# A two-block network on one core: the S5 recurrence over 64 chunks of 8 steps, its matrices formed in the first feed-forward block

## The reference

```
lam_bar = exp(lam * dt);  b_bar = (lam_bar - 1) / lam * B
hs[t] = lam_bar * hs[t-1] + b_bar @ u[t]        # complex, per group
y[t]  = real(C @ hs[t]) + d * u[t]
g = gelu(y);  val, gate = split(g @ w_glu + b_glu);  out = val * sigmoid(gate)
```

## Time and profile before

| | |
|---|---|
| Time, median of 3 runs | 3404.18 us (3403.97 to 3410.24) |
| The profiled execution | 3402.89 us, its span 3401.1 us |
| PE busy | 3106.1 us, 91% of the span |
| DVE, ACT, POOL busy | 1746.6, 1050.0, 1472.9 us |
| Moved by DMA | 280.1 MB, mean 82 GB/s |

### The profile page before, as it was taken

How to read it: one execution, slowest core, us unless ns; L and a number is a source line. 1 busy time by engine, 2 the same in 40 slices (tenths; PEclk the granted TensorE clock), 3 DMA queues, 4 the chain that set the end, 5 groups by cost and what they waited for, 6 DMA issues and landing times. The chain is left out here.

```text
span 3401.1 us, 42283 instructions
## 1 busy us (share of the span) xinstructions
PE 3106.1 (91%) x15056; PEld 2421.5 (71%) x15056; DVE 1746.6 (51%) x2483; ACT 1050.0 (31%) x1419; POOL 1472.9 (43%) x789
## 2 busy tenths in 40 slices
PE   7999989999899999999865556999999999999998
PEld 6859867887687567887643334788887878578887
DVE  4435545647631654656799997522232249432224
ACT  4332223332333534232321121222223344322222
POOL 3324413444433013444356664444443449544443
PEclk9989989999999999999877877999999999999999
DMA  4310003446222114536220000322232230122322
GB/s 126 99 62 1 1 1 124 136 148 235 87 75 87 50 38 136 195 97 228 73 74 1 1 1 10 90 87 91 95 101 75 87 99 14 37 79 95 99 87 74
DMA packets 291923, 280.10 MB, mean 82 GB/s; under 512 B 10832, under 2 KB 275408, under 8 KB 291536
## 3 DMA queue, kind: packets, MB, share of 16 engines
q1 hardware_dynamic: 277968, 227.92, 21.7%
q10 hardware_dynamic: 13824, 50.34, 4.0%
HBM read 276.12 MB, written 2.10 MB: 82 GB/s over the span
## 5 line engine op out<-in xcount | busy, mean ns | idle before, releaser
L232 POOL TENSOR_TENSOR w_lo<-w_raw,w_hi 128x1024 fp32r<-128x1024 f32 x416 | 1040.8, 2524 | 1464.1 <-ACT w_hi L203 1464.1
L242 PE MATMUL bank<-x_hi,w_hi 128*128 128x512 f32 x2048 | 809.6, 395 | 2.5 <-DVE h L401 2.5
L243 PE MATMUL bank<-x_lo,w_hi 128*128 128x512 f32 x2048 | 809.0, 395 | 0.0
L244 PE MATMUL bank<-x_hi,w_lo 128*128 128x512 f32 x2048 | 808.9, 395 | 0.0
L203 ACT ACTIVATE w_hi<-w_raw 128x2048 fp32r<-128x2048 f32 x208 | 398.2, 1915 | 1033.1 <-PE bank L244 871.5
L242 PEld LDWEIGHTS bank<-x_hi,w_hi 128*128 128x128 f32 x2048 | 383.8, 187 | 98.2 <-DVE h L401 3.3
L244 PEld LDWEIGHTS bank<-x_hi,w_lo 128*128 128x128 f32 x2048 | 383.8, 187 | 94.0
L243 PEld LDWEIGHTS bank<-x_lo,w_hi 128*128 128x128 f32 x2048 | 383.9, 187 | 93.7
L1577 PE MATMUL bank<-pr,ck 128*32 128x128 f32 x1024 | 114.8, 359 | 140.7 <-DVE pr L1617 133.4
L1577 PEld LDWEIGHTS bank<-pr,ck 128*32 128x32 f32 x1024 | 92.7, 143 | 176.1 <-DVE pr L1617 146.9
L1146 DVE SCALAR_TENSOR_TENSOR y_gate<-bank,par,y_gate 128x511 f32<-128x511 f32 x88 | 66.0, 749 | 236.4 <-ACT y_gate L1089 230.2
(11 more groups left out here) (398 smaller groups left out, 5178.1 us busy)
## 6 DMA issues: line engine op xcount, KB each, us to landing
w_raw<-in_mlp_w SPq DMA_DIRECT2D x128, 512.0 KB, 4.3
ada_w<-in_ada_w ACTq DMA_DIRECT2D x96, 512.0 KB, 6.3
w_raw<-in_f_w_up SPq DMA_DIRECT2D x88, 512.0 KB, 5.0
w_raw<-in_m_w_in SPq DMA_DIRECT2D x40, 512.0 KB, 4.6
w_raw<-in_a_w_in SPq DMA_DIRECT2D x32, 512.0 KB, 4.9
w_raw<-in_f_w_down SPq DMA_DIRECT2D x32, 512.0 KB, 4.0
w_raw<-in_w_kv SPq DMA_DIRECT2D x16, 512.0 KB, 3.9
w_raw<-in_s_w_glu SPq DMA_DIRECT2D x16, 512.0 KB, 5.2
```

Source lines behind the costliest of these rows:

```text
L232: op = pool.tensor_tensor(w_lo[s][:, part], w_raw[s][:, part], w_hi[s][:, part].bitcast(F32), ALU.subtract)
L242: pe.matmul(dst, hi_l, hi_r, start=start, stop=False)
L243: pe.matmul(dst, hi_l, lo_r, start=False, stop=False)
L244: return pe.matmul(dst, lo_l, hi_r, start=False, stop=stop)
```

## The change

The recurrence is cut into 64 chunks of 8 steps. With P the powers 0 to 8 of lam_bar, three matrices describe a chunk of a group: W (8 x 16 inputs to 64 complex states at the end of the chunk), V (states at its start to 8 x 16 outputs) and T (inputs to outputs inside the chunk, with d on its diagonal).

- **Matrices** are formed in the first feed-forward block in place of the conditioning products: DVE makes V and W for each q (`s_e_dve`, `s_w_dve`), PE transposes W and multiplies for T (`s_build_pe`), ACT copies and stores all three to DRAM (`s_build_act`). Scalars, powers and the fold of C come before, tables of 64 chunks after, between two normalizations of the key/value part (`s_tables_dve`, `s_tables_sp`).
- **S5 part**: each tile of u goes to DRAM and comes back with 8 steps x 16 inputs on the partitions (`s_u_act`, `s_u_sp`). For each q PE forms the chunks' states (`s_z_pe`), DVE rotates, scans once over 512 columns and rotates back, PE adds T u and V s (`s_y_pe`), ACT takes gelu, and y goes through DRAM to the old layout, with tokens ordered by step and chunk (`s_gelu_act`, `s_y_sp`, `s_yh_act`). The parts of q are interleaved with the last `s_in` slots. POOL has no S5 work. W, with its tables, lies in a ring of two buffers.
- **glu**: its first two slots are done together, one tile of g after another (`glu_pe`). DVE adds to h in token order.
- **Conditioning**: i = 0 moves to the second feed-forward block, one or two instructions in each slot, i = 1 to the first MLP (`mlp_dve`, `mlp_act`). Their sums and transposes go between down slots. The attention has 12 matmuls of 512 columns into an unused bank where the sums were.
- Loops of ACT and DVE in these blocks are written out.

```diff
-        def ada_sums_pe(pe, f, first, count):
-
-            if first == 0:
-                pe.wait_ge(ada_used, 48 * (f + 1))
-            for r in range(first, first + count):
-                one = PAR["one_col"] + 31 - r
-                mm = pe.matmul(bank[5 + f][0:32, :], par[:, one:one + 32], ada_acc[:, r // 2, (r % 2) * T:(r % 2) * T + T],
-                               start=(r == 0), stop=(r == 11))
-            if first + count == 12:
-                mm.then_inc(ada_sum, 1)
+        ADA_SUMS, ADA_TURN = bank[6], bank[7]
+
+        def ada_sums_pe(pe, f):
+
+            pe.wait_ge(ada_used, ADA_UNITS * (f + 1))
+            for i in range(3):
+                one = PAR["one_col"] + 31 - i
+                for q in range(4):
+                    r = 4 * i + q
+                    mm = pe.matmul(ADA_SUMS[32 * q:32 * q + 32, :], par[:, one:one + 32], ada_acc[:, r // 2, (r % 2) * T:(r % 2) * T + T],
+                                   start=(i == 0), stop=(i == 2))
+            mm.then_inc(ada_sum, 1)
...
                 if u < 6:
-                    ada_sums_pe(pe, 0, 2 * u, 2)
-                if u == 7:
-                    ada_turn_pe(pe, 0)
+                    for k in range(2):
+                        pe.matmul(bank[5][:, :], ident[:, :], h[:, k, :], start=True, stop=True)
...
+        s5w = nc.dram_tensor("s5w", (S5Q, P, 1536), F32, kind="Internal").ap()
+        s5v = nc.dram_tensor("s5v", (S5Q, P, 1024), F32, kind="Internal").ap()
+        s5t = nc.dram_tensor("s5t", (S5Q, 8, 16, 8, P), F32, kind="Internal").ap()
+        s5u = nc.dram_tensor("s5u", (S5Q, P, T), F32, kind="Internal").ap()
+        s5y = nc.dram_tensor("s5y", (S5Q, 8, 16, 8, 64), F32, kind="Internal").ap()
...
+        def s_e_dve(dve, q):
+
+            ge(dve, b_dve, 2 * q)
+            ge(dve, b_pe, 2 * q - 2)
+            ge(dve, b_sto[q % 2], 48 * (q // 2))
+            dve.wait_ge(s_act, 4 + q + 1)
...
+            s_mark(dve.scalar_tensor_tensor(t0, cr, 1.0, pr, ALU.mult, ALU.mult))
+            a = s_mark(dve.scalar_tensor_tensor(t1, ci, 1.0, pi, ALU.mult, ALU.mult))
+            s_mark(dve.scalar_tensor_tensor(t2, ci, 1.0, pr, ALU.mult, ALU.mult))
+            b = s_mark(dve.scalar_tensor_tensor(t3, cr, 1.0, pi, ALU.mult, ALU.mult))
+            dve.wait_ge(s_dve, a)
+            dve.tensor_tensor(er, kah(t0), kah(t1), ALU.add)
+            dve.wait_ge(s_dve, b)
+            dve.tensor_tensor(ei, kah(t2), kah(t3), ALU.subtract).then_inc(b_dve, 1)
...
+        BUILD = (((0, 0, 0, 0, 0, 0, 0, 0), (1, 2, 1, 2)), ((0, 1, 0, 0, 1, 0, 0, 1), (1, 2, 1, 2)), ((1, 0, 0, 0, 0, 0), (0, 0, 0, 0)))
...
+            first = sum(sum(BUILD[d][p]) for d in range(3) for p in range(2) if (d, p) < (c, part)) + sum(BUILD[c][part][:i])
+            for half in range(first, first + BUILD[c][part][i]):
+                if half % 2 == 0:
+                    s_e_dve(dve, half // 2)
+                else:
+                    s_w_dve(dve, half // 2)
+
+        BUILT_AFTER = {(0, 1, 2): 0, (0, 1, 3): 1, (1, 0, 0): 2, (1, 0, 5): 3, (1, 1, 1): 4, (1, 1, 2): 5, (2, 0, 0): 6, (2, 0, 1): 7}
...
+        def s_build_pe(pe, c, part, i):
+
+            if (c, part, i) not in BUILT_AFTER:
+                return
+            q = BUILT_AFTER[(c, part, i)]
+            pe.wait_ge(b_dve, 2 * q + 2)
+            ge(pe, b_ev, 2 * q)
+            for x in range(2):
+                for k in range(4):
+                    mm = pe.transpose(bank[6 + x][:, k * P:k * P + P], s_w[q % 2][:, x, k, :], ident[:, :])
+            mm.then_inc(b_pe, 1)
+            for x in range(2):
+                for k in range(4):
+                    pe.matmul(bank[4][32 * k:32 * k + 32, 0:P], s_bp[:, x, 4 * q + k, :], s_e[q % 2][:, x, k, 0:P],
+                              start=(x == 0), stop=False)
+            pe.matmul(bank[4][:, 0:16], ident[:, :], par[:, PAR["s5_dm"] + 16 * q:PAR["s5_dm"] + 16 * q + 16],
+                      start=False, stop=True).then_inc(b_pe, 1)
...
+            act.dma_start(s5w[q][:, 0:1024], s_wt[:, :, :, :].rearrange("p x k i -> p (x k i)")).then_inc(b_sto[q % 2], 16)
+            act.dma_start(s5v[q].rearrange("p (j i) -> p j i", i=P),
+                          s_e[q % 2][:, :, :, 16:144].rearrange("p x k i -> p (x k) i")).then_inc(b_sto[q % 2], 16)
+            windows = bass.AP(s_k[q % 2], 0, [[240, P], [16, 8], [1, P]])
+            act.dma_start(s5t[q].rearrange("g h s i -> (g h) s i"), windows).then_inc(b_sto[q % 2], 16)
...
+        def s_tables_sp(sp):
+            sp.wait_ge(s_tab, 1)
+            for x in range(2):
+                sp.dma_start(s5w[:, :, 1024 + 256 * x:1280 + 256 * x].rearrange("q p i -> p q i"),
+                             tab[x][:, :, :].rearrange("p (q k) c -> p q (k c)", k=4)).then_inc(b_sto[0], 16)
...
+        S5_IN = (0, 1, 2, 3, 4, 5, 6, 7)
+        S5_OUT = (0, 1, 2, 3, 6, 7, 4, 5)
+        S5_PE = ("A0", "A1", "A2", "A3", "A4", "A5", "C0", "C1", "A6", "A7", "C2", "C3", "C6", "C7", "C4", "C5")
+
+        def pe_done(step, q):
+
+            return S5_PE.index(f"{step}{q}") + 1
+
+        def s_w_sp(sp, q):
+
+            if q < 2:
+                sp.wait_ge(b_sto[0], S_TABLES)
+                sp.wait_ge(b_sto[1], 48 * 4)
+            else:
+                sp.wait_ge(s_pe, pe_done("A", q - 2))
+                sp.wait_ge(s_st, 2 * q - 2)
+            sp.dma_start(wring[q % 2][:, :], s5w[q]).then_inc(s_wl[q % 2], 16)
...
+        def s_u_sp(sp, q):
+
+            sp.wait_ge(s_put[q % 2], 16 * (q // 2 + 1))
+            if q >= 2:
+                sp.wait_ge(s_get[q % 2], 16 * (q // 2))
+            sp.dma_start(u2[:, q, :, :], s5u[q].rearrange("(g h) (s c) -> (h s) g c", h=16, s=8)).then_inc(s_get[q % 2], 16)
...
+            s_v_sp(sp, 0)
+            s_u_sp(sp, 0)
+            s_u_sp(sp, 1)
+            slot_glu(0)
+            s_v_sp(sp, 1)
+            s_u_sp(sp, 2)
+            s_u_sp(sp, 3)
+            s_w_sp(sp, 2)
+            slot_glu(1)
+            s_w_sp(sp, 3)
+            s_u_sp(sp, 4)
+            s_u_sp(sp, 5)
+            s_w_sp(sp, 4)
+            slot_glu(2)
+            s_w_sp(sp, 5)
+            s_v_sp(sp, 2)
+            s_u_sp(sp, 6)
+            s_u_sp(sp, 7)
+            s_w_sp(sp, 6)
+            s_w_sp(sp, 7)
+            s_v_sp(sp, 3)
+            s_v_sp(sp, 4)
+            s_y_sp(sp, 0)
+            s_v_sp(sp, 5)
+            s_y_sp(sp, 1)
+            s_v_sp(sp, 6)
+            s_y_sp(sp, 2)
+            s_v_sp(sp, 7)
+            s_y_sp(sp, 3)
+            slot_glu(3)
...
+        def s_z_pe(pe, q):
+
+            if q == 0:
+                pe.wait_ge(n_lo, KD * 6)
+            pe.wait_ge(s_get[q % 2], 16 * (q // 2 + 1))
+            pe.wait_ge(s_wl[q % 2], 16 * (q // 2 + 1))
+            ge(pe, s_st, 2 * q - 3)
+            for k in range(4):
                 for x in range(2):
...
+                    for g in range(2):
+                        col = (x * 4 + k) * P + 64 * g
+                        mm = pe.matmul(bank[4 + q % 2][64 * g:64 * g + 64, (x * 4 + k) * 64:(x * 4 + k) * 64 + 64],
+                                       wring[q % 2][:, col:col + 64], u2[:, q, 2 * k + g, :], start=True, stop=True)
+            mm.then_inc(s_pe, 1)
+
+        def s_y_pe(pe, j):
+
+            q = S5_OUT[j]
+            if j == 1:
+                pe.wait_ge(bank_free, 2 * SLOTS["s_glu"])
+            pe.wait_ge(s_st, 2 * q + 2)
+            pe.wait_ge(s_vl[j % 2], 32 * (j // 2 + 1))
+            ge(pe, s_out, j - 1)
...
+            for k in range(4):
+                for g in range(2):
+                    pe.matmul(dst(k, g), tring[j % 4][:, 2 * k + g, :], u2[:, q, 2 * k + g, :], start=(k == 0), stop=False)
+            for k in range(4):
+                for x in range(2):
+                    for g in range(2):
+                        r = slice(64 * g, 64 * g + 64)
+                        mm = pe.matmul(dst(k, g), vring[j % 4][r, x, k, :], s_s[r, q % 6, x, k, :], start=False, stop=(k == 3 and x == 1))
+            mm.then_inc(s_pe, 1)
+
+        def s5_pe(pe, lots):
+            base = SLOTS["s_in"]
+            first_turn(pe, base, x_hi, x_lo, normed(lots), ready_hi=normed_hi(lots))
+            pe_slot_start(pe, base + 2)
+            slot_half(pe, 0, 0, x_hi, x_lo)
+            s_z_pe(pe, 0)
+            s_z_pe(pe, 1)
+            slot_half(pe, 0, 1, x_hi, x_lo)
+            s_z_pe(pe, 2)
+            s_z_pe(pe, 3)
+            pe_slot_start(pe, base + 3)
+            for o in range(2):
+                slot_half(pe, 1, o, x_hi, x_lo)
+            s_z_pe(pe, 4)
+            s_z_pe(pe, 5)
+            s_y_pe(pe, 0)
+            s_y_pe(pe, 1)
+            s_z_pe(pe, 6)
+            s_z_pe(pe, 7)
+            for j in range(2, 8):
+                s_y_pe(pe, j)
+
+        def glu_pe(pe):
+            base = SLOTS["s_glu"]
+            pe.wait_ge(lo_done, base + 2)
+            pe.wait_ge(bank_free, 2 * base)
+            for j, q in enumerate(S5_OUT):
```

(42 more changed lines are left out.)

814 lines of the change are left out of this document (451 added, 363 removed).

## The result

The changed kernel takes 3089.01 us (median of 4 runs, 3087.43 to 3090.79); the kernel before took 3404.07 beside it (3402.75 to 3410.24). The profiled execution has a span of 3085.7 us.

What follows compares the result with a forecast made beforehand. Before S5, a latency chain PE-POOL-DVE of 32 steps bounds, not one full engine; the feed-forward, `glu` and MLP are PE-bound. -283 + 7 + 5 - 3 - 2 + 5 = -271: 3133 us, forecast 3115 to 3150, range 3093 to 3190.

Steps and rivals of the forecast that it cites:

- `s_in` takes 46.7 us of PE as before: In the S5 part's layout: PE's work for `s_in` stays 46.7 us, unchanged by the edit.
- S5, -283: From `s_in`'s first matmul to `glu`'s: `glu` starts at 122 us instead of 405.1, a gain of 283 us.
- with five gaps, 8 us: In S5: PE's gaps lower its clock, about 1.7 us lost after each, 8 us for five.
- The ring of two: In S5: W's load waits for DVE to free one of two buffers; a q takes 7.5 us instead of 6.5.
- rival 3: Everything overlaps: W lands in 4, row halves overlap, few gaps, ring no bound (-10), build 10; 3100 us, chance 0.13.
- `glu`, +7: In `glu`: PE waits for the third slot's weight split, 1.9 us for ACT and 2 x 2.4 for POOL, 7 with semaphores.
- First block, +5: First feed-forward block: 18 us of new PE build work, 13.9 of waits on h mostly gone, 1 more; -3 to +30.
- Second block, -3: Second feed-forward block: 8.7 us of waits go, the sums on PE cost 5 (3 to 10.7); net -3 us.
- Rival 1: The ring and DMA engines bound S5: W lands in 9 or more, PE at 1.2 GHz in gaps; 3175 us, chance 0.25.
- Rival 4: Slower than before: the q's don't overlap, each waiting for its tile's trip through DRAM; 3440 us, chance 0.02.
- Rival 2: The build stalls PE, waiting for DVE's halves and banks, 3 us at each of ten double slots; 3160 us, chance 0.13.
- The 29 us of all 12 splits: In S5: by the skill's lock rule POOL's 12 splits of 2.4 us could hold DVE 29 us; the prediction took 5.

Runs made afterwards that it cites:

- before_shift480: The kernel before with the tiles behind the parameters moved up 480 bytes, to the changed kernel's address 91520, no instruction changed: 3352.07 us.
- after_shift32: The changed kernel with only the arena (x_hi, x_lo, act, m, y) moved up 32 bytes, to 91552: 3144.65 us.
- s5_warm: The changed kernel plus 19 idle fp32 products on PE ahead of z2, z3, z6 and z7: median 3086.17 us, five runs from 3068.06 to 3089.58.
- s5_ring3: The changed kernel with three buffers instead of two for W, cos and sin, and three instead of four for V and T: 3074.81 us.
- no_pe_build: The changed kernel without most of PE's transposes and products that form the S5 matrices in the first feed-forward block: 3085.13 us.

## Why the prediction was right and wrong

**What failed.** "`s_in` takes 46.7 us of PE as before", and with it the same unspoken line for every stage that the change doesn't touch. The sum had only the edited parts. `par` grows by 116 columns (464 bytes), which moves every tile behind it; no term of the prediction is on that. The move is worth -54.3 us on the kernel before (3406.36 beside it to 3352.07) and -55.6 on the changed one (3144.65 to 3089.01). The products that gain are worth 64 us by their count; some of it turns into waits: with the short pitch PE in the old second feed-forward block waits longer for h (8.7 us in the earlier trace rows, 14.4 in before_shift480), and that block gains 3.3 us where its products give 10.

**What the change alone does.** after_shift32 keeps the old distance, so it is what the sum described: 3144.65 us, against 3133 forecast and inside its own 3115 to 3150. Stage by stage, from the start of a norm's last products on PE (L347, in the changed kernel L361) to that of the next, from the profiled executions (before to after_shift32):

| stage | predicted | measured |
|---|---|---|
| S5 with `glu` and what lies ahead | -278 | -264.1 (520.3 to 256.2) |
| first feed-forward block | +5 | +10.6 (395.5 to 406.1) |
| second | -3 | -9.5 (393.1 to 383.6) |
| first MLP | +5 | +4.1 (367.9 to 372.0) |
| the rest | 0 | +2.1 |
| sum | -271 | -256.8 (3401.1 to 3144.3) |

**S5, -283.** It is -274.7 (405.1 to 130.4 in after_shift32). The layout named the right mechanisms, and their sizes were off. The clock: "with five gaps, 8 us" should have been some 20 (the last six y's take 43.3 us, at the 3.86 us of the first they take 23.2). The prediction took the earlier trace rows, where the clock comes back behind a gap with dense 512-column products, as the price of every gap; here z's and y's follow, and it stayed at 0.5 for 58 us, until 3 us into `glu`'s dense products. s5_warm's quick run starts `glu` 19.1 us earlier. W's load lands in 4.4 us instead of 6, and a q of DVE takes 5.36 undisturbed instead of 5.9, both in favour. y's row halves do overlap (3.9 us at full clock instead of 4.5). DVE is done at 1763.7, T = 92.3, where the prediction had 93.5; but `glu` starts 37.6 us later and not 28.5, since all six outputs lie behind z7 and run at 1.2 GHz. The -2 ahead of S5 didn't come: from the norm to the first product of `s_in` it is 20.3 us before and 20.2 in after_shift32.

**The ring of two** was right in kind: s5_ring3 removes all of DVE's later waits. Its price is 14.4 us of `glu`'s start; rival 3 had given it 10.

**`glu`, +7.** The wait is 7.5 us, on POOL, where the prediction put it. The stage grew by 10.6 (90.3 to 100.9 in after_shift32), as the products behind the wait and the first ones of the pass run at the lower clock.

**First block, +5.** 18 - 13.9 + 1: the 18 is 16.7, the 13.9 of waits on h shrank to 1.3 in the changed kernel, but new waits came: 3.1 us for the bank that ACT empties (L1716), 1.7 for POOL, 1.8 for DVE's y_val. From before to after_shift32 PE is busy 17.1 us longer there (376.6 to 393.6) and idle only 6.5 less (18.9 to 12.5), which makes the 10.6. The terms hold as sizes, not as a sum: part of what one wait gives back returns in others and in the clock, as no_pe_build shows.

**Second block, -3.** The waits on h did go, and with them the slow products behind one of them, which no term held. The sums are 2.8 us (L1119), not 5: four column groups overlap.

**Rivals.** Rival 1 fell with its DMA half: W lands in 4.4 us with the DMA engines at 0.73, and S5 reaches 213 GB/s. Its other half, PE at 1.2 GHz for half of S5's products (+25), came nearer to the 20 us that the clock cost than the forecast's 8. Rival 4 was far off. Rival 2's ten stalls didn't come. Rival 3's time, 3100, is nearest to 3089, but that is chance: W in 4 us and the overlapping row halves held, few gaps and a ring that is no bound did not, and the missing 55 us are in none of its terms. That the range of the whole missed by only 4 us is chance too, as two errors of opposite sign met: -55.6 for the pitch and +11.7 for the rest (3144.65 against 3133).

**The signs.** `glu`'s start (129.9 us) lies at the end of the range called right, and the waits between the q's and the one on POOL are as foretold; DVE's 5.36 us a q is under the 6 to 7. Of the signs called wrong one came, a clock near 0.6: 0.51 in the tail.

**On the pages cited.** The loads in 256-byte pieces land in 3.5 (u) and 2.8 us (y), where the 256 KB row of before has 2.6 and the sum had 4.6; the stores ahead of them land in 3.2 and 3.7, where it had 2.6. If the read-modify-write that the Trainium skill's "DMA: Bandwidth & Descriptors" (Specifications) names for pieces under 512 bytes costs anything here, these medians leave it 0.9 us at most.

Four DVE operations were stretched by 1.8 to 2.1 us each beside POOL's splits, 8 us in the stage, where the prediction had 5 (its own half of 12 splits at 1 us is 6, or 0.75 us a q and not 0.6; and of the 0.7 to 0.9 us that it gives for the means of two lines, 0.9 is the scan's median, its mean is 0.6 over its fastest). The trace agrees here with what the Trainium skill's "SBUF — State Buffer" (SBUF: two separate sides) says of the lock: all four have two SBUF inputs, began under a split and ended only behind its end (L2048 at 1714.11, the split at 1713.83), while two beside a split with an input from PSUM kept their 0.69 and 0.68 us. The 29 us of all 12 splits didn't come because only four splits of the stage met such an operation.

## What to carry to other kernels

When a diff changes the size of a tile that is allocated early, list what lies behind it: every address there moves, and that can be worth more than every term of a careful sum but the largest. Give moving and stationary operands a fixed distance on purpose and measure the pitch of the products, from start to start, in a stage that nobody edited. And price a gap of TensorE by what follows it: behind dense 512-column products the clock was back within 3 to 4 us here, while small ones ran on at half of it until the stage ended. The four gaps were 20.2 us together, and the lower clock behind them cost some 20 more.
